# Attention with row maxima of q's high part on two row halves, a ring of seven score banks, and the middle third of prob added up on VectorE

## The reference, cut to what matters

```python
qb = (q * HEAD_DIM ** -0.5)             # 8 heads, 64 wide
s = jnp.einsum('bqkgd,bskd->bkgqs', qblk, k, preferred_element_type=jnp.float32)
p = jax.nn.softmax(s, axis=-1)          # over 2048 latent + 256 context keys
out = jnp.einsum('bkgqs,bskd->bqkgd', p, v)
```

## Time and profile before

| | |
|---|---|
| median of 3 runs | 1492.13 us (1491.62 to 1492.33) |
| the profiled execution's own time | 1492.34 us |
| its span | 1490.5 us |
| PE (TensorE) busy | 1424.3 us, 96% of the span |
| VectorE busy | 792.6 us, 53% |
| ScalarE busy | 599.1 us, 40% |
| GpSimd busy | 709.4 us, 48% |

### The profile page before, as it was taken

One profiled execution on the slowest core, in us unless ns is written; L12 is line 12 of the kernel. 1 busy time (PEld: TensorE's weight loads), 2 busy tenths in 40 slices (PEclk: granted clock), 3 DMA queues, 4 the chain that ended last, 5 costly groups with the idle time before them and its releaser, 6 DMA issues.

```text
span 1490.5 us, 22292 instructions
## 1 busy us (share of the span) xinstructions
PE 1424.3 (96%) x7846; PEld 976.3 (66%) x7846; DVE 792.6 (53%) x1235; ACT 599.1 (40%) x806; POOL 709.4 (48%) x366
## 2 busy tenths in 40 slices
PE   6998986999999999999999999999999999799997
PEld 4677873555555555555555555588888788688886
DVE  2668665656555557656556556531221732555452
ACT  3454321455455445545545546532323133511120
POOL 0324221999999999999999999300000000000000
PEclk9999995999999999999999999999999999999999
DMA  9646326000000000000000000562331051656742
GB/s 367 220 137 194 117 54 209 19 12 22 21 12 20 21 21 12 23 22 11 21 21 11 21 21 11 143 202 92 115 119 49 15 228 61 165 159 210 199 142 84
DMA packets 79364, 134.36 MB, mean 90 GB/s; under 512 B 6077, under 2 KB 53445, under 8 KB 78410
## 3 DMA queue, kind: packets, MB, share of 16 engines
q1 hardware_dynamic: 71914, 120.82, 25.8%
q0 software_dynamic: 6672, 12.58, 3.0%
q10 hardware_dynamic: 720, 0.15, 0.0%
HBM read 103.97 MB, written 29.56 MB: 90 GB/s over the span
## 4 chain that ended last, share of the span: by engine, by line
PE 80%; DVE 2%; DMA 1%; issue 1%; ACT 0%; SPq 0%; POOLq 0%; POOL 0%; ACTq 0%; DVEq 0%
PE pv_ps L1181 17%; PE max_ps L1151 11%; PE s_ps L1167 9%; PE s_ps L1168 9%; PE acc L63 7%; PE acc L64 6%; PE acc L65 6%; PE o_ps L63 4%; PE o_ps L64 4%; PE o_ps L65 4%; PE row_ps L1189 1%; DMA gin<-rest_scratch 1%; DVE chunk_max L1062 0%; DVE w_o_lo L1689 0%; DVE w_o_raw L1661 0%
## 5 line engine op out<-in xcount | busy, mean ns | idle before, releaser
L967 POOL TENSOR_TENSOR prob_sum<-prob_sum,prob 128x1024 f32<-128x1024 f32 x217 | 520.8, 2400 | 33.5 <-ACT prob L1006 17.4
L1062 DVE TENSOR_REDUCE chunk_max<-max_ps 128x1 f32<-128x512 f32 (+1 forms) x640 | 393.0, 636 | 257.2 <-PE max_ps L1151 254.1
L1006 ACT ACTIVATE prob<-s_ps 128x1024 f32<-128x1024 f32 x288 | 295.0, 1025 | 300.0 <-PE s_ps L1168 288.1
L1181 PE MATMUL pv_ps<-prob,v 128*32 128x512 f32 x2304 | 266.9, 596 | 0.0
L1151 PE MATMUL max_ps<-k_hi,blk_q_hilo 128*128 128x512 f32 (+1 forms) x640 | 247.1, 404 | 12.7 <-DMA blk_q_hilo<-q_scratch 10.2
L1167 PE MATMUL s_ps<-blk_q_hilo,k_hi 128*128 128x512 f32 x576 | 233.8, 406 | 1.7 <-DVE blk_q_negm L1075 0.9
L1168 PE MATMUL s_ps<-blk_q_negm,k_lo 68*128 68x512 f32 x576 | 229.5, 398 | 0.0
L1151 PEld LDWEIGHTS max_ps<-k_hi,blk_q_hilo 128*128 128x128 f32 x640 | 120.4, 192 | 102.7 <-issue 38.5
L1181 PEld LDWEIGHTS pv_ps<-prob,v 128*32 128x32 f32 x2304 | 65.1, 109 | 137.8 <-issue 134.0
L63 PE MATMUL acc<-hh,w_rest_hi 128*128 128x512 f32 x384 | 151.1, 393 | 0.2 <-ACTq L1490 0.2
L64 PE MATMUL acc<-hl,w_rest_hi 128*128 128x512 f32 x384 | 150.4, 392 | 0.0
(11 more groups left out here) (266 smaller groups left out, 1867.5 us busy)
## 6 DMA issues: line engine op xcount, KB each, us to landing
xt_raw<-in_xt SPq DMA_DIRECT2D x16, 512.0 KB, 5.3
x_tok<-in_x SPq DMA_DIRECT2D x16, 512.0 KB, 4.9
blk_q_hilo<-q_scratch SPq DMA_DIRECT2D x32, 256.0 KB, 2.7
h_raw<-in_xg SPq DMA_DIRECT2D x4, 2048.0 KB, 9.9
rest_scratch<-stage SPq DMA_DIRECT2D x32, 256.0 KB, 2.2
gin<-rest_scratch SPq DMA_DIRECT2D x16, 512.0 KB, 10.7
x_res<-in_x SPq DMA_DIRECT2D x16, 512.0 KB, 3.7
out_x<-res SPq DMA_DIRECT2D x16, 512.0 KB, 3.0
```

Of the source, the lines that this page charges most:

```text
L967: nc.gpsimd.tensor_tensor(acc_pool[slot][:], acc_pool[slot][:], probs(slot, j)[:], ALU.add).then_inc(s_psum, 1)
L1006: nc.scalar.activation(probs(slot, j)[:], s_ps[slot2(slot, j)][:], ACT.Exp).then_inc(s_exp, 1)
L1062: nc.vector.reduce_max(chunk_max[:, qt, kc:kc + 1], max_ps[u % 2][:, 0:MAX_CHUNKS[kc]], X_AXIS).then_inc(s_mfree, 1)
L1181: last = nc.tensor.matmul(pv_ps[row:row + QUAD], k.v[:, 2 * j + e, kvh, half * QUAD:(half + 1) * QUAD], probs(slot, j)[:, e * QB:(e + 1) * ...
```

## The change

The two `max_ps` banks and the two double banks `s_ps`, with the bank `row_ps`, become a ring of seven single banks that maxima and scores share. A new buffer `q_max` per slot holds q's high part on both partition halves, filled by two more DMAs per block. A maximum product now contracts over 64 partitions only: products for even key chunks use the lower half of the rows, those for odd chunks the upper half, and the two of a pair write different banks. The 256 context keys of all four query tiles go into two banks (two products each), each reduced by one instruction. Maxima are no longer interleaved one by one with scores: they are issued as four groups of four plus the context group, score tiles as groups of six. ScalarE exponentiates one tile (512 columns) per instruction, 18 per block. The maximum is that of the high part alone. The buffers of `prob` 3, 4 and 5 are added on VectorE (`middle_sum`), and GpSimd adds that sum in (`join`): 6 adds of its own per block where there were 8. `prob_sum` moves from behind the first third of the values to behind the second, and `copy_den` with it. In `tail` one semaphore is folded into another.

```diff
@@ TensorE @@
-            def max_use(b, slot, kvh, u):
-                qt, kc = divmod(u, len(MAX_CHUNKS))
...
-                pe.wait_ge(s_mfree, b * MAX_USES + (u + 1))
...
-                nc.tensor.matmul(max_ps[u % 2][:, 0:MAX_CHUNKS[kc]], q_hilo[slot][:, qt * P:(qt + 1) * P],
-                                 k.k_hi2[:, kvh, key0:key0 + MAX_CHUNKS[kc]], start=True, stop=True).then_inc(s_mfull, 1)
+            def max_context(b, slot, kvh):
+                for q in range(Q_TILES):
+                    half = q % 2
+                    rows = slice(half * HD, (half + 1) * HD)
+                    last = nc.tensor.matmul(ring[half][:, q // 2 * CTX:(q // 2 + 1) * CTX],
+                                            q_max[slot][rows, q * P:(q + 1) * P], k.k_hi2[rows, kvh, SEQ:KEYS],
+                                            start=True, stop=True)
+                last.then_inc(s_mfull, 1)
+            def max_chunks(b, slot, kvh, q):
+                banks = BEHIND if q % 2 else AHEAD
+                for c in range(CHUNKS):
...
+                    rows = slice(c % 2 * HD, (c % 2 + 1) * HD)
+                    last = nc.tensor.matmul(ring[banks[c]][:], q_max[slot][rows, q * P:(q + 1) * P],
+                                            k.k_hi2[rows, kvh, c * QB:(c + 1) * QB], start=True, stop=True)
+                    if c % 2:
+                        last.then_inc(s_mfull, 1)
...
             def body(b, slot, kvh, next_kvh, later_kvh):
-                phase(0, b, slot, kvh, b + 1, 1 - slot, next_kvh)
+                scores(b, slot, kvh, 1, next_kvh is not None)
+                if next_kvh is not None:
+                    max_chunks(b + 1, 1 - slot, next_kvh, 2)
                 value_products(b, slot, kvh, 0)
-                if not isinstance(b, int) or b:
-                    pe.wait_ge(s_psum, b * POOL_OPS + POOL_OPS)
-                    prob_sum(acc_pool[1 - slot])
-                phase(1, b, slot, kvh, b + 1, 1 - slot, next_kvh)
+                if next_kvh is not None:
+                    max_chunks(b + 1, 1 - slot, next_kvh, 3)
+                scores(b, slot, kvh, 2, next_kvh is not None)
                 if next_kvh is not None:
                     turn_max(b + 1)
                 value_products(b, slot, kvh, 1)
-                phase(2, b + 1, 1 - slot, next_kvh, b + 2, slot, later_kvh)
+                if not isinstance(b, int) or b:
+                    if next_kvh is not None:
+                        pe.wait_ge(s_row, b + 2)
...
+                    pe.wait_ge(s_psum, b * POOL_OPS + POOL_OPS)
+                    prob_sum(acc_pool[1 - slot])
+                if later_kvh is not None:
...
+                    max_context(b + 2, slot, later_kvh)
+                if next_kvh is not None:
+                    scores(b + 1, 1 - slot, next_kvh, 0, later_kvh is not None)
+                if later_kvh is not None:
+                    max_chunks(b + 2, slot, later_kvh, 0)
                 value_products(b, slot, kvh, 2)
+                if later_kvh is not None:
+                    max_chunks(b + 2, slot, later_kvh, 1)
@@ VectorE @@
+            def reduce_context(b):
+                for half in range(2):
+                    dve.wait_ge(s_mfull, b * MAX_FULL + 1)
+                    pair = ring[half][:].rearrange("p (a n) -> p a n", a=2)
+                    nc.vector.reduce_max(chunk_max[:, half::2, CHUNKS], pair, X_AXIS).then_inc(s_mfree, 1)
...
+            def middle_sum(b, slot):
+                dve.wait_ge(s_psum, b * POOL_OPS + 3)
+                dve.wait_ge(s_exp, b * KT + 10)
+                nc.vector.tensor_tensor(acc_dve[:], probs(slot, 3)[:], probs(slot, 4)[:], ALU.add).then_inc(s_dsum, 1)
+                dve.wait_ge(s_dsum, b * DVE_OPS + 3)
+                dve.wait_ge(s_exp, b * KT + 12)
+                nc.vector.tensor_tensor(acc_dve[:], acc_dve[:], probs(slot, 5)[:], ALU.add).then_inc(s_dsum, 1)
...
                 negate(b + 1)
+                middle_sum(b, slot)
                 max_rows(b + 1, 1 - slot)
@@ GpSimd @@
+            def join(b, slot):
+                pool.wait_ge(s_dsum, b * DVE_OPS + 2 * DVE_OPS)
+                pool.wait_ge(s_psum, b * POOL_OPS + (POOL_OPS + 2))
+                nc.gpsimd.tensor_tensor(acc_pool[slot][:], acc_pool[slot][:], acc_dve[:], ALU.add).then_inc(s_psum, 1)
...
                     combine(b - 1, 1 - slot)
-                for j in range(3, PAIRS):
+                join(b, slot)
+                for j in range(6, PAIRS):
                     add(b, slot, j)
@@ ScalarE @@
-                nc.scalar.activation(probs(slot, j)[:], s_ps[slot2(slot, j)][:], ACT.Exp).then_inc(s_exp, 1)
+                for e in range(2):
...
+                    bank = ring[SCORE_BANKS[(2 * j + e) % GROUP_TILES]]
+                    nc.scalar.activation(probs(slot, j)[:, e * QB:(e + 1) * QB], bank[:], ACT.Exp).then_inc(s_exp, 1)
@@ SyncE @@
+            def load_max(b, slot):
+                for half in range(2):
+                    sp.dma_start(q_max[slot][half * HD:(half + 1) * HD].bitcast(F32), q_v[b][0:HD]).then_inc(s_qm[slot], 16)
```

216 lines of the change are left out of this document (128 added, 88 removed).

## The result

| | before | with the change |
|---|---|---|
| median | 1491.9 us (1491.62 to 1492.33) | 1473.07 us (1471.7 to 1474.11) |
| span of the profiled execution | 1490.5 us | 1472.3 us |
| PE busy | 1424.3 us | 1388.5 us |
| VectorE busy | 792.6 us | 835.6 us |
| GpSimd busy | 709.4 us | 557.5 us |

The change takes 0.9878 of the time before, 95% interval 0.9862 to 0.9894: 19 us less, about half of the 39 that were forecast, and inside the range. The first two fences are from the page of the profile of the change: the busy times, then the costliest groups, with busy time and mean in ns, then the idle time ahead of them and what ended it.

The account below looks back on a forecast made before the run. TensorE was taken to bound the kernel. Per body -2.11 + 0.1 + 0.85 - 0.09 = -1.25 over 30.5 bodies gave -38; with -3.4 at the start and +2 at the end, -39.5: 1453 us, range 1435 to 1483.

Parts of the forecast that it names:

- I count 0: In each body, the sum of prob waits for max_rows behind VectorE's adds: possibly 0.3 us late, counted as 0.
- the 2 us allowed for the end: In the last two blocks, ScalarE's 16 steps for the tail delay exponentials that TensorE needs: 2 us of loss.
- inner one of 1437 to 1472: Range around the forecast, from free borders to pairs of 0.30 or 0.3 us of waits; chance 0.65.
- dearer borders: Rival: the five new borders cost 0.35 us each, a body takes 21.7 us, 1480 us in all; chance 0.10.
- Overlap of the halves: Maxima in each body: a pair on two row halves costs 0.2335 us, like one product; 2.11 us saved.
- The efficiency of 77%: Estimate for maxima from the skill's 3.07x for four products: a pair costs 0.30 us, about 17 us more in the end.
- The rival of halves in turn: Maxima pairs do not overlap and cost 0.467 us each; body 22.8 us, 1514 us in all; chance 0.11 for slower.
- Borders: Changes of array shape in each body: five new ones at 0.17 us each, 0.85 us added.
- Body without waits: One pass of the attention loop takes 20.8 us instead of 22.05, with nothing counted for new waits.
- Start: First block, bound by VectorE: with seven banks the reductions run without mutual waits with TensorE, 3.4 us saved.
- free borders: Low end of the inner range: new shape changes cost nothing, -26 us, less half of that for new waits.
- The rival of collisions: In the loop, VectorE's adds meet busy GpSimd and lose 0.86 us per body, 26 us, giving 1479 us; chance 0.10.

Follow-up runs that it names:

- e4: The change with all maxima of 512 keys on the lower row half, so these products cannot overlap: 1519.93 us, 1.0214 of the kernel before.
- e5: The change with q_max holding high and low parts and all maxima contracting over 128 rows: 1502.36 us, 1.0089 of the kernel before.
- e1: The change with max_rows ahead of the two adds of middle_sum on VectorE: 1464.24 us, 0.9824 of the kernel before.
- e6: The change with GpSimd adding all nine buffers again and VectorE none: 1454.28 us, 0.9762 of the kernel before.
- e7: The change with the edits of e1, e2 and e3 together: 1460.68 us, 0.9801 of the kernel before.
- e3: The change with the four h_normed steps spread singly over bodies 0, 1, 14 and 15, behind reduce_context: 1467.68 us, 0.9848 of the kernel before.
- e2: The change with the last block's VectorE adds no longer waiting for GpSimd's last three adds: 1471.76 us, 0.9874 of the kernel before.
- the repeat: The change as it is, measured once more: 1472.51 us, 0.9878 of the kernel before.
- e9: The change with 32 products of unused result among the first block's maxima: 1469.72 us, 0.9879 of the kernel before.
- e8: The change with the edits of e1 and e3, and GpSimd joining VectorE's sum last, behind buffers 6, 7 and 8: 1560.16 us, 1.0472 of before.
- e11: The change with the edits of e6, e3 and e9 together: 1453.95 us, 0.9738 of the kernel before.

## Why the prediction had the gain twice too large

The forecast was 1453 us, 39 less than before; it became 1473.07, 19 less. What TensorE's own work costs was forecast rightly. What failed is the step "I count 0" for the new wait of the sum for VectorE (10 to 11 us), the steps of `h_normed`, which are in no term, and the 2 us allowed for the end (7.0 measured in the last block alone). The time lies inside the range of 1435 to 1483 us, but just outside the inner one of 1437 to 1472, and its upper part was there for dearer borders and for collisions, neither of which happened in the loop.

**Overlap of the halves: right.** I took 0.2335 us for a pair. The records of a pair start 3 to 8 ns apart (505.107 and 505.110, then 505.441 and 505.449), and e4 prices the overlap at 0.46 us per group, all that there was to gain. The efficiency of 77% that I had worked out from the Trainium skill ("TensorE: Matmul & The Clock Gate", Part 3, measured speedup) would have made a pair 0.30 us; by the rows it is 0.23, so the measurement decides against my estimate. The page's figure is for four groups of 32 rows, and carrying it over to two of 64 was my step. The rival of halves in turn has its price about right, 22.8 us forecast for its body and 22.72 measured in e4 (where the context pairs still overlap and the sum still waits, which nearly cancel), but it is not what happens.

**Borders: right.** Forecast 0.17 us each; measured 0.18 over all eleven (20.74 us less 18.73 of pieces without borders: 8.41 scores, 2.11 maxima, 7.71 values, 0.43 sum, 0.07 turn), and 0.19 for the five new ones (e5 against e4). The rule of the Trainium skill ("TensorEngine Tiling (Array Packing)", key properties), that a change of mode drains TensorE, fits these numbers, and by e5 against e4 a change between full and half height costs as much as one to the narrow shape.

**Body without waits: right.** 20.8 forecast, 20.74 measured in e1, e6 and e7. The loop of e7, 641.3 us, is within 3 us of the forecast 643.9 (681.9 less 38). ScalarE's share of the body was put too high, 12.8 us where it is 11.2, which changed nothing.

**"I count 0" for VectorE: wrong, 10 to 11 us.** I had found that adds and row need 3.1 us beside 2.8 us of values, and put the missing 0.3 down to reductions that might end earlier. They do: the negation ends at 518.76, 0.51 us before the values start. But from there to the sum (522.23) adds, row and their handovers take 3.47 us, not 3.1, and there is room for 0.51 + 2.60 = 3.11. That leaves the 0.36. Of a margin near zero I counted only the kind side; with the 0.3 us that my own working gave, the forecast would have been 9 us nearer.

**Bodies 14 and 15: missing, 4 us.** The rows of `h_normed` stood in the earlier trace rows, but I used them only as a price for collisions and never asked what the steps themselves do in front of reductions that TensorE now waits for. Before the change the same steps cost 0.3 us in two bodies. e3 settles that they are the cause; e6 shows that it is not the adds beside them.

**End: wrong, 5 us over the 2 allowed.** I looked for late exponentials. They exist, but in block 29, where they cost 1.25 us and count in the loop's line; the 7.0 us of the last block are another wait. The sum of `prob` in the loop was early, as I said, but the last block's adds wait for all of GpSimd's, and there the 5 us that GpSimd idles ahead of `join` are on the path. e6 shows it by taking the cause away (12.89 us); e2, which only took the wait, ran into the collision. The +1.9 us of the rest is not a loss by itself: the repeat has 534.12 us there, with the same wait and 3.1 us of products at the lower clock behind it.

**Start: wrong, 2.6 us.** 3.4 forecast, 0.8 found. VectorE did its part: its negation comes 15.9 us after the start of attention where it came after 18.4, 2.5 us earlier. Of these, 1.7 are lost between there and the first values. I had counted VectorE's reductions alone, but in this profile TensorE, which waits for VectorE again and again here, is at its lower level of 1.2 GHz for the whole start (0.51 from 228 to 262 us); before, it rose 26.2 us after the start, ahead of the first values (0.59). The profiles of one and the same start, with the rise at 20.8 to 33.9 us, lie 3.6 us apart (e9), so the clock is enough to explain the missing part, and it took another 1.1 us in body 0. What sets the moment of its rise was not tried apart.

By the table, the loop is 13.3 us over its forecast, the last block 5.0, the rest 1.9 and the start 2.6. Less the 1.6 that the stages ahead were shorter by chance, that makes up the 21 us between forecast and profile. Of these, the 1.9 and the 1.1 of body 0 are chance too, as far as the repeat shows.

Two bounds of the inner range do not follow from their own terms: half of the 26 us for free borders gives 1440 us, not 1437, and pairs of 0.30 (16 us) or waits of 0.3 us (9 us) give 1469 or 1462, not 1472. The wait of 0.3 us in it is close to what was found, 0.36 us a body. The rival of collisions gave 1479 us, 6 from what was measured, through another mechanism: in the loop the adds last 1.23 us, as forecast, so it isn't what happened there.

## What to carry to other kernels

Work that is taken off a busy engine isn't a gain by itself: ask first whether that engine would still fit into the shorter body (here 20.3 of 20.7 us), and only then pay for the queue, the join and the order that the move needs. Where a step is put in front of one that the bounding engine waits for, count the margin even when it is a few tenths, since it returns in each body. And follow every wait once through the last pass of the loop, where slack in the steady state can be on the path.

## What was not expected of the hardware

- Two fp32r products of 64 rows on different row halves start 3 ns apart and together cost one. Their loads too: four loads of 64x128 take 0.30 us, where two of 128x128 took as long.

```profile
522.80 0.30 PEld L1198 LDWEIGHTS ring_ps<-k_hi,blk_q_max 64*128 64x128 f32 x4 [0.41 <-issue]
```

- VectorE and GpSimd adds that meet lengthen each other by far more than I had allowed: 1.23 to 3.20 us (e8), 1.21 to 3.40 and 2.28 to 4.47 (e2), while three GpSimd adds, 7.45 us in the change's last block, take 9.01 and 10.13. The Trainium skill ("SBUF — State Buffer", the shared port) has the lock; the rows show its price, and that an idle gap on one engine can be worth more than the time it seems to waste.
- A wait of TensorE can cost more than itself: behind 1.42 us (e8) and 1.12 us (e6) the granted clock was 0.50 for 3.4 us, which costs another 1.7 us.
- With the same code at the start of attention, the first values came 28.0 to 31.6 us after it in different kernels' profiles, at a mean granted clock of 0.51 to 0.65 from 228 to 262 us. With products that nobody needs it was 0.91 (e9) and 0.85 (e11), and the medians didn't move by what could be measured.
